# Second feed-forward up product: four of eight slabs as seven block products

## The reference

```python
h = _modulate(_rmsnorm(x, g_ffn[l]), sh2, sc2)
a = jnp.square(jax.nn.relu(jnp.einsum('bsd,df->bsf', h, w_ff1[l])))
x = x + gt2[:, None, :] * jnp.einsum('bsf,fd->bsd', a, w_ff2[l])
```

## Time and profile before

| | |
|---|---|
| median of 3 runs | 1674.01 us (1673.73 to 1674.56) |
| the profiled execution: its time | 1675.87 us |
| its span in the trace | 1673.1 us |
| PE busy in the span | 1646.5 us, 98% |
| DVE, ACT, POOL busy | 1111.6, 726.9, 165.3 us |
| ff1b, as it runs | from 431.6 to 518.7 us of the span |

### The profile page before, as it was taken

The page is one execution under the profiler, slowest core; times in us unless marked ns, Lnnn a source line. Parts: engine busy times, 40 slices in busy tenths (PEclk is TensorE's granted clock), DMA queues, the critical chain, the costliest instruction groups (busy, mean ns, idle before and its releaser), DMA issues.

```text
span 1673.1 us, 19977 instructions
## 1 busy us (share of the span) xinstructions
PE 1646.5 (98%) x7759; PEld 1314.4 (79%) x7759; DVE 1111.6 (66%) x1407; ACT 726.9 (43%) x1011; POOL 165.3 (10%) x158
## 2 busy tenths in 40 slices
PE   6999999999999999999999999999999999999999
PEld 3888778888888887887666788886678888888887
DVE  2888888532454577786999864548868886642364
ACT  2443334221222235646888523538832355431241
POOL 0005100000000000000455200004610000000000
PEclk9999999999999999999999999999999999999999
DMA  9544322222222242222111222221022222222222
GB/s 376 200 187 175 150 76 95 81 101 101 101 101 91 88 149 76 101 76 101 51 51 54 80 94 99 70 102 50 1 101 101 101 101 91 88 99 101 101 101 101
DMA packets 25422, 174.17 MB, mean 104 GB/s; under 512 B 2800, under 2 KB 3184, under 8 KB 5104
## 3 DMA queue, kind: packets, MB, share of 16 engines
q1 hardware_dynamic: 21440, 146.52, 24.4%
q10 hardware_dynamic: 3888, 26.38, 4.0%
HBM read 168.69 MB, written 4.19 MB: 103 GB/s over the span
## 4 chain that ended last, share of the span: by engine, by line
PE 83%; DVE 10%; ACT 5%; issue 1%; DMA 1%; ACTq 0%; POOL 0%; SPq 0%; DVEq 0%; POOLq 0%
PE bank L1608 25%; PE bank L1610 25%; PE bank L1609 25%; ACT p L381 3%; DVE p L1285 2%; DVE w_lo L863 2%; PE bank L2137 1%; PE bank L2163 1%; PE bank L2149 1%; DMA x<-x_in 1%; PE bank L1839 1%; DVE clipped L1259 1%; PE bank L1821 1%; PE bank L1657 1%; DVE t L962 1%
## 5 line engine op out<-in xcount | busy, mean ns | idle before, releaser
L1608 PE MATMUL bank<-h,w_hi 128*128 128x512 f32 x1184 | 465.5, 393 | 1.6 <-DVE w_lo L863 0.9
L1610 PE MATMUL bank<-h,w_lo 128*128 128x512 f32 x1184 | 460.9, 389 | 0.0
L1609 PE MATMUL bank<-h,w_hi 128*128 128x512 f32 x1184 | 460.8, 389 | 0.0
L381 ACT ACTIVATE w_hi<-raw 128x2048 fp32r<-128x2048 f32 (+1 forms) x129 | 246.6, 1912 | 312.4 <-DMA raw<-slabs 308.5
L863 DVE TENSOR_TENSOR w_lo<-raw,w_hi 128x2048 fp32r<-128x2048 f32 (+1 forms) x129 | 298.4, 2313 | 88.6 <-ACT w_hi L381 84.8
L1608 PEld LDWEIGHTS bank<-h,w_hi 128*128 128x128 f32 x1184 | 222.3, 188 | 49.2 <-issue 2.9
L1609 PEld LDWEIGHTS bank<-h,w_hi 128*128 128x128 f32 x1184 | 222.4, 188 | 47.1 <-issue 1.4
L1610 PEld LDWEIGHTS bank<-h,w_lo 128*128 128x128 f32 x1184 | 222.2, 188 | 46.4
L1608 PE MATMUL bank<-a_hi,w_hi 128*128 128x512 f32 x432 | 168.1, 389 | 0.3 <-DVE x L1537 0.3
L1610 PE MATMUL bank<-a_hi,w_lo 128*128 128x512 f32 x432 | 168.1, 389 | 0.0
L1609 PE MATMUL bank<-a_lo,w_hi 128*128 128x512 f32 x432 | 168.0, 389 | 0.0
(11 more groups left out here) (355 smaller groups left out, 2408.3 us busy)
## 6 DMA issues: line engine op xcount, KB each, us to landing
raw<-slabs SPq DMA_DIRECT2D x127, 1024.0 KB, 4.8
ada_chunk<-ada ACTq DMA_DIRECT2D x24, 1024.0 KB, 6.9
x<-x_in SPq DMA_DIRECT2D x4, 1024.0 KB, 9.1
spill_x<-x SPq DMA_DIRECT2D x1, 2048.0 KB, 10.5
x<-spill_x SPq DMA_DIRECT2D x2, 1024.0 KB, 6.0
out<-x SPq DMA_DIRECT2D x8, 256.0 KB, 2.0
raw<-slabs SPq DMA_DIRECT2D x2, 768.0 KB, 4.2
inv<-inv ACTq DMA_DIRECT2D x1, 1024.0 KB, 7.1
```

The source lines that it names most:

```text
L381: return act.activation(out, in_, f, **kw)
L1608: pe.matmul(out, w[0], a[0], start=start, stop=False)
L1609: pe.matmul(out, w[0], a[1], start=False, stop=False)
L1610: return pe.matmul(out, w[1], a[0], start=False, stop=stop)
```

## The change

Number the slabs of ff1b 0 to 7. Slabs 0, 2, 4 and 7 stay plain: 48 matmuls of 512 columns. Slabs 1, 3, 5 and 6 (`SEVEN`) are seen as a 2 x 2 block product: the weights' quarters (512 columns of the slab each: two output tiles by two halves of k) times the two halves of k and the two halves of the tokens. That would be eight block products; seven are done, of sums and differences of blocks. One block product is 4 k-steps x 3 = 12 matmuls of 256 columns, so a slab has 84 of them.

- POOL makes sums of the tokens once, in ff2a (`whole`, then four mixed halves), and for each of the four slabs four sums of weight quarters: s1, s2, s4 and a difference (`weight_sums`). ACT makes the high parts (`mixed_heads`, `plain_head`, `sum_heads`), DVE the low parts (`mixed_tails`, `sum_tails`).
- DVE puts the four result quarters together from the seven products with six additions of 256 columns (`seven_sums`, `last_sum`); ACT copies product 2.
- relu, square and high part are now all on ACT (`a_head`, one slab late), the low part on DVE (`a_low`).
- The products of ff1b go round all eight banks (`seven_bank`). Product i waits until the bank of product i-8 has been read (`seven_bank_free`).
- The first tile of ff2b waits for `a` in pairs (`k | 1`), as the tiles of a pair come in reversed order.
- The semaphores of several one-time events elsewhere are merged (two softplus stages, roots, `consts_in` with `gate_w_in`); the instructions there stay as they are.

Product numbers: (n, j) is product j of slab n; a plain slab has j = 0 and 1 (its two tiles), a seven-slab j = 0 to 6. The core of the diff:

```diff
+HALF = S // 2
+SEVEN = (1, 3, 5, 6)
+OWN_BANKS = ("uq_0", "uq_1", "ukv", "ff1b")
...
+    products = [(n, nth) for n in range(8) for nth in range(7 if n in SEVEN else 2)]
+    def seven_bank(n, nth):
+        return banks[(products.index((n, nth)) + 4) % 8][:, 0:HALF if n in SEVEN else S]
...
+    def seven_bank_free(n, nth):
+        if nth == 2 or n not in SEVEN:
+            return "first_taken", taken_by_act(n, nth)
+        return "seven_read", 6 * SEVEN.index(n) + (1, 3, 0, 2, 4, 5, 6)[nth]
...
-            sp.dma_start(gw[:], gate_w_d).then_inc(sem("gate_w_in"), 16)
+            sp.dma_start(gw[:], gate_w_d).then_inc(sem("consts_in"), 16)
...
+            def mixed_heads():
+                act.wait_ge(sem("sums_made"), 4)
+                for n, (place, src) in enumerate([(mix_hi[:, n, :, :], mix_raw[:, n, :, :]) for n in range(4)]):
+                    do.tell(fn(place, src, ACT.Copy), "seven_head", n + 1)
+            def plain_head(n):
+                s, i = SLAB0["ff1b"] + n, SEVEN.index(n)
+                act.wait_ge(sem(f"raw_in{s % SLOTS}"), 16 * (s // SLOTS) + 16)
+                act.wait_ge(sem("tile_done"), 2 * (s - SLOTS) + 2)
+                do.tell(fn(quarter(w_hi, n, 0, 2), quarter(raw, n, 0, 2), ACT.Copy), "seven_head", 4 * i + 5)
+            def sum_heads(n):
+                s, i = SLAB0["ff1b"] + n, SEVEN.index(n)
+                for nth, which in enumerate(("s2", "s1")):
+                    act.wait_ge(sem("sums_made"), 4 * i + 6)
+                    f, lo, hi = sum_place(n, which)
+                    do.tell(fn(hi, f, ACT.Copy), "seven_head", 4 * i + 6 + nth)
+                act.wait_ge(sem("sums_made"), 4 * i + 8)
+                do.tell(fn(quarter(w_hi, n, 2, 2), quarter(raw, n, 2, 2), ACT.Copy), "seven_head", 4 * i + 8)
+                f, lo, hi = sum_place(n, "s4")
+                do.tell(fn(hi, f, ACT.Copy), "w_head", s + 1)
+            def a_head(nth):
+                n, t = nth // 2, nth ^ 1
+                a = a_raw[:, t, :]
+                if n in SEVEN:
+                    act.wait_ge(sem("seven_read"), 6 * SEVEN.index(n) + 5 + nth % 2)
+                    do(fn(a, a, ACT.Relu))
+                else:
+                    act.wait_ge(sem("tile_done"), 2 * (SLAB0["ff1b"] + n) + 2)
+                    do.tell(fn(a, seven_bank(n, t % 2), ACT.Relu), "first_taken", taken_by_act(n, t % 2))
+                do(fn(a, a, ACT.Square))
+                do.tell(fn(a_hi[:, t, :], a, ACT.Copy), "a_head", nth + 1)
+            def seven_out(n):
+                if n + 1 in SEVEN:
+                    plain_head(n + 1)
+                else:
+                    weight_head(SLAB0["ff1b"] + n + 1)
+                if n in SEVEN:
+                    act.wait_ge(sem("seven_done"), 6 * SEVEN.index(n) + 3)
+                    do.tell(fn(a_raw[:, 2 * n, left], seven_bank(n, 2), ACT.Copy), "first_taken", taken_by_act(n, 2))
+                if n + 1 in SEVEN:
+                    sum_heads(n + 1)
+                if n:
+                    a_head(2 * n - 2)
+                    a_head(2 * n - 1)
...
+                if half:
+                    for n in range(8):
+                        seven_out(n)
+                    a_head(14)
+                    a_head(15)
+                    weight_head(SLAB0["ff2b"] + 1)
...
+                    if half == 0 and n == 5:
+                        mixed_heads()
...
+            def lows(lo, src, hi):
+                return dve.tensor_tensor(lo, src, hi.bitcast(f32), ALU.subtract)
+            def mixed_tails():
+                for n, (lo, src, hi) in enumerate([(mix_lo[:, n, :, :], mix_raw[:, n, :, :], mix_hi[:, n, :, :]) for n in range(4)]):
+                    dve.wait_ge(sem("seven_head"), n + 1)
+                    do.tell(lows(lo, src, hi), "seven_split", n + 1)
+            def sum_tails(n, parts):
+                i = SEVEN.index(n)
+                for part in parts:
+                    if part < 2:
+                        dve.wait_ge(sem("sums_made"), 4 * i + 4 + (3, 2)[part])
+                        dve.wait_ge(sem("seven_head"), 4 * i + 6 + part)
+                        f, lo, hi = sum_place(n, ("s2", "s1")[part])
+                        do.tell(lows(lo, f, hi), "seven_split", 4 * i + 5 + part)
+                    elif part < 4:
+                        first = 2 * (part - 2)
+                        dve.wait_ge(sem("sums_made"), 4 * i + 8)
+                        dve.wait_ge(sem("seven_head"), 4 * i + (5, 8)[part - 2])
+                        do.tell(lows(quarter(w_lo, n, first, 2), quarter(raw, n, first, 2), quarter(w_hi, n, first, 2)),
+                                "seven_split", 4 * i + 5 + part)
+                    else:
+                        dve.wait_ge(sem("w_head"), SLAB0["ff1b"] + n + 1)
+                        f, lo, hi = sum_place(n, "s4")
+                        do.tell(lows(lo, f, hi), "w_split", SLAB0["ff1b"] + n + 1)
+            def a_low(nth):
+                t = nth ^ 1
+                dve.wait_ge(sem("a_head"), nth + 1)
+                do.tell(lows(a_lo[:, t, :], a_raw[:, t, :], a_hi[:, t, :]), "a_ready", 16 + nth + 1)
+            def last_sum(n):
+                dve.wait_ge(sem("tile_done"), 2 * (SLAB0["ff1b"] + n) + 2)
+                c12 = a_raw[:, 2 * n, right]
+                do.tell(dve.tensor_tensor(c12, seven_bank(n, 6), c12, ALU.add), "seven_read", 6 * SEVEN.index(n) + 6)
+            def seven_sums(n):
+                c11, c12, c21, c22 = (a_raw[:, 2 * n + m, side] for m in range(2) for side in (left, right))
+                seven = n in SEVEN
+                i = SEVEN.index(n) if seven else 0
+                if n - 1 in SEVEN:
+                    last_sum(n - 1)
+                if n > 1:
+                    a_low(2 * n - 4)
+                    a_low(2 * n - 3)
+                if seven:
+                    dve.wait_ge(sem("first_taken"), taken_by_act(n, 2))
+                    dve.wait_ge(sem("seven_done"), 6 * i + 1)
+                    do.tell(dve.tensor_tensor(c12, seven_bank(n, 0), c11, ALU.add), "seven_read", 6 * i + 1)
+                if n + 1 in SEVEN:
+                    sum_tails(n + 1, range(3))
+                else:
+                    weight_tail(SLAB0["ff1b"] + n + 1)
+                if seven:
+                    dve.wait_ge(sem("seven_done"), 6 * i + 4)
+                    do.tell(dve.tensor_tensor(c21, seven_bank(n, 3), c12, ALU.add), "seven_read", 6 * i + 2)
+                    do(dve.tensor_tensor(c22, seven_bank(n, 1), c21, ALU.add))
+                    do.tell(dve.tensor_tensor(c12, seven_bank(n, 1), c12, ALU.add), "seven_read", 6 * i + 3)
+                if n + 1 in SEVEN:
+                    sum_tails(n + 1, range(3, 5))
+                if seven:
+                    dve.wait_ge(sem("seven_done"), 6 * i + 5)
+                    do.tell(dve.tensor_tensor(c11, seven_bank(n, 4), c11, ALU.add), "seven_read", 6 * i + 4)
+                    dve.wait_ge(sem("seven_done"), 6 * i + 6)
+                    do.tell(dve.tensor_tensor(c21, seven_bank(n, 5), c21, ALU.add), "seven_read", 6 * i + 5)
...
+                    if name == "ff2a" and m == 4:
+                        mixed_tails()
...
+                if half:
+                    for n in range(8):
+                        seven_sums(n)
+                    for nth in (12, 13):
+                        a_low(nth)
+                    weight_tail(SLAB0["ff2b"] + 1)
+                    for nth in (14, 15):
+                        a_low(nth)
...
-            pool.wait_ge(sem("total_ready"), 1)
+            pool.wait_ge(sem("a_ready"), 16)
+            for part in (low_k, high_k):
+                do(pool.tensor_tensor(whole[:, part, :], h_hi[:, part, :].bitcast(f32), h_lo[:, part, :].bitcast(f32), ALU.add))
+            m1, m2, m3, m4 = (mix_raw[:, n, :, :] for n in range(4))
+            do.tell(pool.tensor_tensor(m1, whole[:, low_k, right], whole[:, low_k, left], ALU.subtract), "sums_made", 1)
+            do.tell(pool.tensor_tensor(m3, whole[:, high_k, right], whole[:, low_k, right], ALU.subtract), "sums_made", 2)
+            do.tell(pool.tensor_tensor(m2, whole[:, high_k, right], m1, ALU.subtract), "sums_made", 3)
+            do.tell(pool.tensor_tensor(m4, whole[:, high_k, left], m2, ALU.subtract), "sums_made", 4)
+            def weight_sums(n):
+                s, i = SLAB0["ff1b"] + n, SEVEN.index(n)
+                pool.wait_ge(sem(f"raw_in{s % SLOTS}"), 16 * (s // SLOTS) + 16)
+                if i == 0:
+                    pool.wait_ge(sem("seven_split"), 4)
+                    pool.wait_ge(sem("tile_done"), 2 * SLAB0["ff1b"])
+                elif n != 6:
+                    pool.wait_ge(sem("tile_done"), 2 * (SLAB0["ff1b"] + SEVEN[i - 1]) + 2)
+                (s1, _, _), (s2, _, _), (s4, _, _) = (sum_place(n, which) for which in ("s1", "s2", "s4"))
+                q11, q12, q21, q22 = (quarter(raw, n, q) for q in range(4))
```

(86 more changed lines are left out.)

94 lines of the change are left out of this document (63 added, 31 removed).

## The result

The changed kernel takes 1676.5 us (median of 22 runs) against 1673.94 us for the kernel before: ratio 1.0015, 95% interval 1.0009 to 1.0022, so 1.5 to 3.7 us more. One of the 22 runs was disturbed (1839.7 us at a mean granted clock of 0.85) and is left out of the ratio. The profiled execution took 1676.07 us with a span of 1674.1 us.

The account below looks back on a forecast made before the run. PE was taken to bound ff1b and ff2b, so only its matmuls and waits count: -3.2 saving + 4.3 stop at (5, 6) + 0.6 into ff2b = +1.7, 1675.7 us; forecast's own range 1673.1 to 1677.2, with rivals 1671.8 to 1679.0.

Parts of the forecast that it names:

- Saving: Slabs 1, 3, 5 and 6 of ff1b: 10.08 us instead of 10.88 each, 4 x 0.80 = 3.2 us less.
- Exposed weight loads: Seven-slabs: by the skill's formula 36 more exposed loads per slab would cost 15 us; put aside on the trace's 0.120 us.
- Work beside PE costs nothing: Token sums on POOL, 20 to 38 us, and added ACT and DVE work hide under ff2a's 87 us: nothing.
- Slabs 1, 3 and 5: ff1b: their sums come in time, slack 1.0 us before product (3, 6); cost nothing, up to 0.5 us if late.
- The stop at (5, 6): ff1b, slab 5: PE waits for the bank of (4, 0) behind POOL's sums and ACT's steps, 4.2 + 0.1 us.
- 7.2 to 8.6, I take 8.3: When POOL's difference for slab 6 is made, in us from slab 5's first matmul; 7.2 if undisturbed by DVE.
- 2.9 + 0.1 if nothing disturbs POOL: Size in us of PE's stall plus restart at product (5, 6) if POOL's sums run undisturbed.
- Into ff2b: Start of ff2b, k = 14: PE waits for the last a_low pair, 0.5 + 0.1 = 0.6 us (0 to 1.2).
- POOL and DVE in each other's way throughout: Rival: POOL sums take 2.25 us, (3, 6) waits too, slab 5 costs 6.1 us; +4.0, 1678.0 us. Chance 0.19.
- No stop: Rival: the bank wait at (5, 6) costs 1.5 us at most; 1670.8 to 1672.6 us. Chance 0.10.
- Dearer products over the whole phase: Rival: seven-slab products do not stream at 0.120 us; at 0.13 us 3.4 us are lost, 1679.1 and more. Chance 0.06.
- if products keep another pace: Sign that the prediction is wrong: products not keeping the forecast pace, seven-slabs of 10.1 us apart from stalls.

Follow-up runs that it names:

- relus_first: Changed kernel, but in slab 5 ACT empties both banks of slab 4 before waiting for slab 6's sums: 1672.01 us, ratio 0.9988 to the kernel before.
- pool_more: Changed kernel with POOL making s4 of slab 6 twice, one more instruction of 1.29 us behind product (5, 1): ff1b 91.04 us in one execution.
- kept_busy_13: Changed kernel with 13 unread matmuls of 128 columns on PE ahead of product (5, 6): 1675.16 us, ratio 1.0005 to the kernel before.
- relus_tail: relus_first, and DVE makes the last two a_low ahead of the weight_tail of ff2b's second slab: 1670.90 us, ratio 0.9983 to the kernel before.
- before_idle3: Kernel before, with PE made to wait at slab 5 of ff1b for three POOL memsets: idle 3.35 us, ff1b 92.26 us in one execution.

## Why the prediction held, and where its terms were off

The time was forecast at 1675.7 us, +1.7, and came out at 1676.5, +2.6 by the medians, inside the forecast's own range and within what was called no change. The mechanism was right: a saving, eaten by a stop at (5, 6) and a small one in ff2b. One size was wrong and one term was missing, and they nearly cancelled, so that the time came out this close is partly luck.

- **Saving.** 0.80 us per slab were forecast; the runs give 3.14 / 4 = 0.785. The 256-column stream of rows 4 carried over with its roles swapped. Exposed weight loads, weighed in the prediction and put aside, did not show: PE was busy throughout the 83.90 us, with loads beside it for 76.35.
- **Work beside PE costs nothing.** Right: relus_first shows it with the same instructions. The token sums took from 346.24 to 371.4 us of the span, 25 us (20 to 38 forecast), and were done long before ACT took them at 393.7. That the merged semaphores cost nothing was not tested by itself.
- **Slabs 1, 3 and 5.** No wait, as forecast. Slab 3's difference was made at 457.65, which is 6.4 us into slab 2 (7.6 forecast, 5.7 at best).
- **The stop at (5, 6).** The place and the chain were right, and pool_more confirms the link to POOL. The size was 3.13 + 0.08 us instead of 4.2 + 0.1. The step that was off is "7.2 to 8.6, I take 8.3": the difference was made at 7.21. I let DVE's low parts push POOL back. But `sum_tails` waits for s4 before it takes s2's low part, so that can only compete with the difference, which POOL begins at the same moment; POOL was first by 0.01 us, and DVE waited. In all six traces of kernels with the slabs 5 and 6 side by side POOL's three sums took 1.29 to 1.31 us. The seven ACT steps behind it took 4.4 us as worked out. The prediction's "2.9 + 0.1 if nothing disturbs POOL" is a slip in its own terms: 7.2 + 4.4 + 0.1 - 8.64 = 3.1, and 3.2 with the restart, which is what was measured.
- **The low clock.** This term was missing. I priced the stop with its own length and a restart of 0.1 us, since the kernel before shows clock 1.00 throughout. It costs 1.48 us more, by kept_busy_13 against the changed kernel. The two errors are of opposite sign: forecast 4.3, measured 3.2 + 1.5 = 4.7. With POOL's chain estimated rightly and the clock still left out, the forecast would have been 1.1 us lower, 1674.6, and farther from 1676.5.
- **Into ff2b.** 0.6 us forecast, 0.63 measured; relus_tail removes all of it.
- **The sum.** -3.14 + 3.21 + 1.48 + 0.63 = +2.2 us, which are the two stages' 88.58 + 87.67 against 2 x 87.04. The medians differ by 2.6; the other 0.4 us are not located, and the interval of the ratio covers them.
- **The rivals.** POOL and DVE in each other's way throughout: no, POOL's sums for the weights were 1.29 to 1.62 us long, not 2.25; only two of the token sums in ff2a, which nobody waits for, were as slow (4.35 us for 1024 columns, 2.17 per 512). No stop: no. Dearer products over the whole phase: no. What I named as the point that would break the forecast, "if products keep another pace", did happen, for 3.4 us.

## What to carry to other kernels

A saving on the bound engine is worth its price only if every buffer that its stream needs comes free in time: go through the lists of the engines that free them, and where one of them first waits for something late, ask who needs what stands behind that wait. Here two instructions moved ahead of a wait turned 2.6 us lost into 2.0 gained, and another swap into 3.1. A stop of TensorE in a dense stream can cost more than its length: here stops of 2.2 us and more did, those of 0.3 to 0.8 us did not. If it cannot be removed, matmuls into a free bank can fill it, but they must end with it: 24 of them ran 2.0 us over and lost more than they gained. And when a ring of buffers gets another length, look again at which user the next phase inherits a buffer from.

## What the runs showed of the hardware

- After PE idled 2.19, 2.97 or 3.35 us within a stream in which it had been busy without a break, the granted clock went from 1.00 to 0.50 (2.4 to 1.2 GHz) for 3.4 us, starting about 0.5 to 1.4 us after work had resumed. With 4.35 us idle (pool_more) it fell about 1.0 us before work resumed and stayed low for 6.8 us. After 0.79 us it did not fall. The price beside the stop was 1.5 to 1.8 us for the 3.4 us, whatever the length of the stop in that range.
- Not every stop of such a length brings it. At the start of the kernel PE stands three times in 17 us, for 6.99, 2.89 and 2.90 us, in the kernel before (7.03, 2.83 and 2.83 in the changed one), between short pieces of work. The granted clock is 1.00 from 0 to 50 us, and the eight matmuls of 512 columns behind a stop take 1.93 us together, the pace of the full clock. PE's two longest entries in the waits of the kernel before:

```profile
PE bank L1737 <- DMA ada_chunk<-ada: 9.9, 2, 7.0
PE bank L1657 <- ACT sq L381: 2.9, 1, 2.9
```

  What tells these stops from the one in the dense stream, no run here shows.
- It can also come without a single long stop. The profiled execution of relus_first has such a time at the start of attention, where PE works in short pieces and in the 15 us before never waits longer than 0.76 us; the kernel before, with the same code, has none there:

```profile
1142.00:1148.00 6.00, 5.27 (x20) 2.72 (x19) 5.40 (x17) 5.07 (x14) 1.54 (x5) 0.98 0.10 44
1148.00:1151.50 3.50, 3.50 (x15) 2.87 (x14) 2.00 (x7) 2.15 (x7) 2.39 (x5) 0.55 0.03 5
```

  The traces of relus_tail, pool_more and before_idle3 have it at the same place, the other six do not, and before_idle3 has no seven-slab; so the change does not bring it. Why it comes in some executions and not in others stays open. Three of the 21 runs of the changed kernel had a mean clock of 0.998 instead of 0.999, and took 1677.8 to 1677.9 us, 1.4 over the median; and 5 of the 22 runs of relus_first and relus_tail have 0.999 instead of 1.000.
- POOL and DVE really take turns. The Trainium skill ("SBUF — State Buffer", Who interferes with whom) says that a DVE instruction with two SBUF inputs contends with a GpSimd instruction that reads SBUF, and that the order of issue decides who is blocked. The trace agrees: POOL's difference, begun 0.01 us earlier, kept its 1.29 us, and DVE's low part ended 0.55 us behind it. The sum of both lengths would be 1.98 us and DVE took 1.83, so it did not wait for quite all of POOL's 1.29.
